# Splitting the weights of a woven projection in one piece instead of four quarters

## The reference

```python
def mem_cross_attention(q, mem_n, w_mkv):          # second block, once in each of its two layers
    k, v = jnp.split(mem_n @ w_mkv, 2, axis=-1)    # mem_n 256 x 1024, w_mkv 1024 x 1024
    ...

def swa_sink_attention(q, k, v, sinks):            # first block, layer 1: 12 heads, 4 blocks of 128 tokens
    s = jnp.einsum('bnqhgd,bnkhd->bnhgqk', qb, kband).astype(jnp.float32) * (dh ** -0.5)
    s = jnp.where(valid[None, :, None, None, :, :], s, -jnp.inf)
    m = jnp.maximum(jnp.max(s, axis=-1, keepdims=True), sink)
    p = jnp.exp(s - m)
    p = p / (jnp.sum(p, axis=-1, keepdims=True) + jnp.exp(sink - m))
    o = jnp.einsum('bnhgqk,bnkhd->bnqhgd', p.astype(v.dtype), vband)
```

## Time and profile before

| what | value |
|---|---|
| runs, median (lowest to highest) | 2280.4 us (2272.93 to 2281.29), 3 runs |
| profiled execution, its own time | 2280.4 us |
| its span in the profile | 2278.9 us |
| TensorE busy | 93% of the span |
| VectorE busy | 51% |
| ScalarE busy | 39% |
| chain that ended last, by engine | PE 77%, DVE 15%, ACT 6%, issue 1% |
| mean granted TensorE clock | 0.958 |
| sliding stage in the trace | about 795 to 934 us |

### The profile page before, as it was taken

How to read it: one execution, slowest core, us unless ns; L and a number is a source line. 1 busy time by engine, 2 the same in 40 slices (tenths; PEclk the granted TensorE clock), 3 DMA queues, 4 the chain that set the end, 5 groups by cost and what they waited for, 6 DMA issues and landing times.

```text
span 2278.9 us, 24588 instructions
## 1 busy us (share of the span) xinstructions
PE 2111.9 (93%) x9984; PEld 1716.7 (75%) x9984; DVE 1168.8 (51%) x2252; ACT 883.9 (39%) x1565; POOL 231.7 (10%) x155
## 2 busy tenths in 40 slices
PE   6998899999997999999999999999998899799787
PEld 6986688888786777788887878878776666577575
DVE  5325453333226666453332237998865248655553
ACT  5336443222124356442322222477451222456520
POOL 1000010000002000010000003766500000000000
PEclk9998599999998999999999999999999899999998
DMA  6330022233233212222222322322322312011211
GB/s 225 114 117 11 10 83 93 93 99 105 102 107 114 67 55 75 93 97 98 93 93 93 111 93 96 108 74 74 102 74 74 110 56 70 23 38 56 74 56 56
DMA packets 28800, 192.60 MB, mean 85 GB/s; under 512 B 3264, under 2 KB 3408, under 8 KB 7440
## 3 DMA queue, kind: packets, MB, share of 16 engines
q1 hardware_dynamic: 24848, 175.96, 22.5%
q0 software_dynamic: 3264, 12.99, 1.7%
q10 hardware_dynamic: 576, 2.10, 0.2%
HBM read 186.84 MB, written 4.19 MB: 84 GB/s over the span
## 4 chain that ended last, share of the span: by engine, by line
PE 77%; DVE 15%; ACT 6%; issue 1%; DMA 0%; POOL 0%; SPq 0%; DVEq 0%; POOLq 0%; ACTq 0%
PE bank L390 22%; PE bank L391 21%; PE bank L392 21%; DVE bank L1971 4%; PE bank L1660 2%; DVE WL L362 1%; PE bank L1551 1%; ACT WH L348 1%; PE bank L1090 1%; PE bank L1648 1%; PE bank L1099 1%; PE bank L1027 1%; PE bank L1561 1%; PE bank L2112 1%; PE bank L1653 1%
## 5 line engine op out<-in xcount | busy, mean ns | idle before, releaser
L390 PE MATMUL bank<-XH,WH 128*128 128x512 f32 (+1 forms) x1504 | 598.5, 398 | 25.4 <-DVE XL L551 10.3
L392 PE MATMUL bank<-XH,WL 128*128 128x512 f32 (+1 forms) x1504 | 568.5, 378 | 0.0
L391 PE MATMUL bank<-XL,WH 128*128 128x512 f32 (+1 forms) x1504 | 567.9, 378 | 0.0
L362 DVE TENSOR_TENSOR WL<-RAW,WH 128x2048 fp32r<-128x2048 f32 x128 | 293.2, 2291 | 462.8 <-ACT WH L348 462.8
L348 ACT ACTIVATE WH<-RAW 128x2048 fp32r<-128x2048 f32 x148 | 282.3, 1908 | 347.1 <-PE bank L392 341.7
L390 PEld LDWEIGHTS bank<-XH,WH 128*128 128x128 f32 x1504 | 286.8, 191 | 94.6 <-issue 24.7
L391 PEld LDWEIGHTS bank<-XL,WH 128*128 128x128 f32 x1504 | 287.1, 191 | 54.4 <-issue 5.6
L392 PEld LDWEIGHTS bank<-XH,WL 128*128 128x128 f32 x1504 | 286.3, 190 | 53.3 <-issue 0.6
L1971 DVE SCALAR_TENSOR_TENSOR bank<-conv_in,cols,bank 128x512 f32<-128x512 f32 x290 | 198.1, 747 | 1.1
L390 PE MATMUL bank<-WH,XH 128*128 128x512 f32 (+2 forms) x416 | 154.6, 372 | 9.8 <-DVE XL L551 6.3
L391 PE MATMUL bank<-WL,XH 128*128 128x512 f32 (+2 forms) x416 | 153.7, 369 | 0.0
(11 more groups left out here) (316 smaller groups left out, 3023.8 us busy)
## 6 DMA issues: line engine op xcount, KB each, us to landing
RAW<-weights SPq DMA_DIRECT2D x164, 1024.0 KB, 4.9
row_a<-rows POOLq DMA_DIRECT2D x7, 512.0 KB, 5.8
row_b<-rows POOLq DMA_DIRECT2D x6, 512.0 KB, 6.0
x_res<-x SPq DMA_DIRECT2D x1, 2048.0 KB, 16.7
kv<-mem_park POOLq DMA_DIRECT2D x2, 1024.0 KB, 5.1
out<-x_res ACTq DMA_DIRECT2D x4, 512.0 KB, 2.6
mem_tok<-mem SPq DMA_DIRECT2D x1, 1024.0 KB, 5.0
mem_tok<-mem POOLq DMA_DIRECT2D x1, 1024.0 KB, 8.4
```

The costliest lines, as they stand in the source:

```text
L362: dve.tensor_tensor(WL[j][:, :], RAW[j][:, :], WH[j][:, :].bitcast(F32), ALU.subtract).then_inc(*lo.mark())
L390: pe.matmul(ps, ah, bh, start=first, stop=False)
L391: pe.matmul(ps, ah, bl, start=False, stop=False)
L392: return pe.matmul(ps, al, bh, start=False, stop=last)
```

## The change

The quarters are no longer used in this stage. `split_act` and `lower_dve`, one whole operation each, take their place, at the entry at which the unit ends: the last of 18 entries for keys and the last but one of 16 for values, since the empty entry now stands behind each step of the values. The list keeps its 136 entries, and they alone are dealt out over the same 66 steps. The copies of the values move from an odd entry to the even one before it. The lags stay, and so do the lines that do the work. The quarters of a later stage (`gate_b`) are not touched.

```diff
-    VALUE_STEPS = 2 * KB
-    BESIDE = [(layer, unit, k) for layer in range(2) for unit in range(4)
-              for k in range(FEATURE_STEPS if unit < 2 else VALUE_STEPS)]
-    QUARTERS = {}
-    for e, (layer, unit, k) in enumerate(BESIDE):
-        if k == (FEATURE_STEPS if unit < 2 else VALUE_STEPS) - 1:
-            for q in range(4):
-                QUARTERS[e + 1 + 2 * q] = q
+    BESIDE_VALUES = [step for i in range(2) for t in range(MEMT) for q in range(4) for step in ((i, t, q), None)]
+    BESIDE = [(layer, part, k) for layer in range(2) for part, count in (("keys", 2 * FEATURE_STEPS), ("values", len(BESIDE_VALUES)))
+              for k in range(count)]
     BESIDE_LAGS = 2, 3
-    BESIDE_ENTRIES = max(QUARTERS) + 1
 
     def beside(n, lag=0):
 
-        steps, n = len(SLIDE_ORDER) - BESIDE_LAGS[1], n - lag
-        return range(BESIDE_ENTRIES * n // steps, BESIDE_ENTRIES * (n + 1) // steps) if 0 <= n < steps else []
+        steps = len(SLIDE_ORDER)
+        n = n - lag
+        at = [0] + [len(BESIDE) * (k + 1) // (steps - BESIDE_LAGS[1]) for k in range(steps - BESIDE_LAGS[1])] + [len(BESIDE)] * 8
+        return BESIDE[at[n]:at[n + 1]] if n >= 0 else []
...
-    def beside_act(e):
-        if e in QUARTERS:
-            split_quarter_act(QUARTERS[e])
-        if e >= len(BESIDE):
-            return
-        layer, unit, k = BESIDE[e]
-        u = U["mem2_kv", layer, unit]
-        if unit < 2 and k in (KB, FEATURE_STEPS - 1):
-            c = k // (FEATURE_STEPS - 1)
...
+    def beside_act(layer, part, k):
+        if part == "keys":
+            unit, k = divmod(k, FEATURE_STEPS)
+            u = U["mem2_kv", layer, unit]
+            for c in range(2):
+                if k == KB * (c + 1) + c:
...
+            if k == FEATURE_STEPS - 1:
+                split_act()
+        elif BESIDE_VALUES[k]:
+            i, t, q = BESIDE_VALUES[k]
+            if (i, q) == (1, 3):
...
+            if (t, q) == (MEMT - 1, 3):
+                split_act()
+
+    def beside_dve(layer, part, k):
+        if part == "keys" and k % FEATURE_STEPS == FEATURE_STEPS - 1:
+            lower_dve()
+        elif part == "values" and BESIDE_VALUES[k] in [(0, MEMT - 1, 3), (1, MEMT - 1, 3)]:
+            lower_dve()
```

More of the change, by code:

```diff
@@ L1445, in band, with beside_pe @@
         return P if t == 0 else 2 * P
-    VALUE_STEPS = 2 * KB
-    BESIDE = [(layer, unit, k) for layer in range(2) for unit in range(4)
-              for k in range(FEATURE_STEPS if unit < 2 else VALUE_STEPS)]
-    QUARTERS = {}
-    for e, (layer, unit, k) in enumerate(BESIDE):
-        if k == (FEATURE_STEPS if unit < 2 else VALUE_STEPS) - 1:
-            for q in range(4):
-                QUARTERS[e + 1 + 2 * q] = q
+    BESIDE_VALUES = [step for i in range(2) for t in range(MEMT) for q in range(4) for step in ((i, t, q), None)]
+    BESIDE = [(layer, part, k) for layer in range(2) for part, count in (("keys", 2 * FEATURE_STEPS), ("values", len(BESIDE_VALUES)))
+              for k in range(count)]
     BESIDE_LAGS = 2, 3
-    BESIDE_ENTRIES = max(QUARTERS) + 1
     def beside(n, lag=0):
-        steps, n = len(SLIDE_ORDER) - BESIDE_LAGS[1], n - lag
-        return range(BESIDE_ENTRIES * n // steps, BESIDE_ENTRIES * (n + 1) // steps) if 0 <= n < steps else []
-    def beside_pe(e):
-        if e >= len(BESIDE):
-            return
-        layer, unit, k = BESIDE[e]
-        u = U["mem2_kv", layer, unit]
[L1472 to L1477, removed]
+        steps = len(SLIDE_ORDER)
+        n = n - lag
+        at = [0] + [len(BESIDE) * (k + 1) // (steps - BESIDE_LAGS[1]) for k in range(steps - BESIDE_LAGS[1])] + [len(BESIDE)] * 8
+        return BESIDE[at[n]:at[n + 1]] if n >= 0 else []
+    def beside_pe(layer, part, k):
+        if part == "keys":
+            unit, k = divmod(k, FEATURE_STEPS)
+            feature_step_pe(k, U["mem2_kv", layer, unit], n=MEM, source=m2_parts, ring="beside")
+        elif BESIDE_VALUES[k]:
+            i, t, q = BESIDE_VALUES[k]
+            u, kb, high, low = U["mem2_kv", layer, 2 + i], 4 * i + q, *m2_parts
+            if (t, q) == (0, 0):
                 PE.wait_ge("split_lo", u + 1)
@@ L1481, in beside_pe @@
             mm = three_passes(bank[banks_of["mem2_v", layer, t]][:, :], high[:, kb, t * P:(t + 1) * P],
-                              low[:, kb, t * P:(t + 1) * P], WH[u % 2][:, s], WL[u % 2][:, s], kb == 0, kb == KB - 1)
+                              low[:, kb, t * P:(t + 1) * P], WH[u % 2][:, 512 * q:512 * q + 512],
+                              WL[u % 2][:, 512 * q:512 * q + 512], kb == 0, kb == KB - 1)
+            last = (t, q) == (MEMT - 1, 3)
             if kb == KB - 1:
-                mm.then_inc(*(used if t == MEMT - 1 else T).mark("full", "mem2_v", layer, t))
-            elif (t, q) == (MEMT - 1, 3):
+                mm.then_inc(*(used if last else T).mark("full", "mem2_v", layer, t))
+            elif last:
@@ L1510, in beside_dve @@
-    def beside_dve(e):
-        if e in QUARTERS:
-            lower_quarter_dve(QUARTERS[e])
+    def beside_act(layer, part, k):
+        if part == "keys":
+            unit, k = divmod(k, FEATURE_STEPS)
+            u = U["mem2_kv", layer, unit]
+            for c in range(2):
+                if k == KB * (c + 1) + c:
+                    if layer:
+                        ACT.wait_ge(*after("park", 0, "keys"))
+                    ACT.wait_ge(*after("full", u, c))
+                    act.activation(m2_keys[:, MEM * (2 * unit + c):MEM * (2 * unit + c + 1)], bank_of(u, c)[:, 0:MEM],
+                                   AF.Copy).then_inc(*A.mark("emptied", u, c))
+            if k == FEATURE_STEPS - 1:
+                split_act()
+        elif BESIDE_VALUES[k]:
+            i, t, q = BESIDE_VALUES[k]
+            if (i, q) == (1, 3):
+                if layer:
+                    ACT.wait_ge(*after("park", 0, "values"))
+                ACT.wait_ge(*after("full", "mem2_v", layer, t))
+                act.activation(m2_values[:, 512 * t:512 * t + 512], bank_of("mem2_v", layer, t)[:, :], AF.Copy).then_inc(
+                    *A.mark("emptied", "mem2_v", layer, t))
+            if (t, q) == (MEMT - 1, 3):
+                split_act()
@@ L1536, in sliding_pe @@
                 if stream == 1:
-                    beside_pe(other[k])
+                    beside_pe(*other[k])
                     continue
@@ L1584, in sliding_act @@
             for other in beside(n, BESIDE_LAGS[0]):
-                beside_act(other)
+                beside_act(*other)
     def sliding_dve():
@@ L1612, in sliding_dve @@
             for other in beside(n, BESIDE_LAGS[1]):
-                beside_dve(other)
+                beside_dve(*other)
             if n % 3 == 2 and n < 12:
```

## The result

The change costs 3.5%: 2355.5 us in the median (2347.4 to 2366.3, 4 runs) where the kernel before took 2276.8 (4 runs); the ratio is 1.035, with a 95% interval of 1.029 to 1.041. The prediction was 2295 us, with a range of 2286 to 2302. The sign was right, and the loss of 78.7 us is over five times the 14.6 that I forecast.

What follows compares the result with a forecast made beforehand. TensorE bounds the sliding stage. To 2280.4 us the prediction added 10.3 us net (12.9 of stalls less 2.6 back) and 4.8 us for falls of the clock: 2295 us, range 2286 to 2302.

Steps and rivals of the forecast that it cites:

- The bound: In the sliding stage TensorE is busy 134.5 of 137.0 us; VectorE and ScalarE have over a third of their time free.
- The lump's way to TensorE: ScalarE's whole split, then VectorE's whole operation, delay the reciprocal that TensorE's transposes await; beside keys 0.88 us late.
- Step 11: First whole operation on VectorE, ahead of a rotation, beside memory jobs: TensorE stalls 2.0 us.
- Step 20: Second place on VectorE, first token block with small jobs: TensorE stalls 2.5 us.
- Step 35: Fourth place on VectorE, beside keys: a stall of 0.88 us plus 0.48 for a copy of values, 1.4 us.
- VectorE's wait for ScalarE: VectorE idles 0.2 to 1.2 us ahead of its whole operation until ScalarE's split is ready.
- The sum of the stalls: Seven TensorE stalls ahead of its transposes in the sliding stage, 12.9 us together.
- Step 68: Last place, behind the last result, beside the transposes of `mixed`: no stall; 1.2 us if VectorE can't catch up.
- What comes back: TensorE's waits for last quarters and a reciprocal go, 1.7 us, plus savings at the stage's end: 2.6 us back.
- The clock: Four falls to half clock behind the stalls, 1.2 us each: 4.8 us; ends 0 and 12 us.
- Longer falls of the clock: Rival: half clock lengthens a step and light work keeps it low; 2303 us, chance 0.06.
- The count of short idle times: In the earlier trace five of six idle times of 2.2 to 2.5 us brought half clock, none of 1.3 to 1.5.

Runs made afterwards that it cites:

- four_whole_late: Whole operations at the last five places only (steps 35, 44, 53, 60, 68), against lists_quarters: 2280.7, 2317.7, 2331.6 and 2332.3 us.
- vector_whole: VectorE's operations whole at the place of the fourth quarter, ScalarE's splits in quarters except the last, against lists_quarters: 2354.0 us, ratio 1.033.
- lists_quarters: The changed kernel's list and pace, with quarters put back on both engines at seven of the eight places (the last stays whole): 2278.3 us, ratio 0.999.
- warm_memory: The kernel before plus 16 useless 512-column multiplies, four ahead of each of the first four jobs of the first layer's memory attention: 2277.0 us, ratio 0.999.
- pure_stall: lists_quarters plus two useless subtractions on VectorE at the end of step 21: 2320.8 us, ratio 1.018.
- one_whole_early: Against lists_quarters, also whole: ScalarE's split in step 19 and VectorE's operation in step 20, beside values: 2341.5 us, ratio 1.029.

## Why the prediction was wrong

- **The bound.** Right. TensorE sets the stage (busy 209.8 of 215 us), and VectorE's and ScalarE's free time is not the question.
- **The lump's way to TensorE.** Right, wherever the clock was at full. Step 11: 2.0 forecast, 2.15 measured. Step 20: 2.5 and 2.19. Step 35: 1.4 and, in four_whole_late, 1.25. VectorE's wait for ScalarE ahead of its operation: 0.2 to 1.2 forecast, 0.51 and 0.99 measured. Without ScalarE's lateness (vector_whole) 1.5 worked out and 1.34 measured.
- **The sum of the stalls.** 12.9 us forecast, 4.3 measured in the stage, wrong as a consequence of the clock: of seven stalls two happened. The other five found steps of 4.0 us in place of 2.2, in which the same late reciprocal is early. No run shows what the seven would have cost at full clock.
- **Step 68.** Costed at nothing, 1.2 us at worst. Wrong: TensorE stood 2.21 us there in lists_quarters and in the kernel after, and 2.1 us came of it against quarters at full clock (warm_memory). Against the profile of before it doesn't show, since that had half clock there.
- **What comes back.** 2.6 us forecast, and right in kind: the waits for WL are gone, the wait for the last result is 0.38 us in place of 0.78, and with quarters the new list's stage is 3.5 us shorter in one profile.
- **The clock.** This is the step that failed: "I take four falls. Each loses 3.0 x (1 - 9/14) = 1.1 us, a little more with its edges". That the clock falls behind a stall of 2 us was right, in both places. What a fall costs I took from the earlier trace rows, where dense multiplies of 512 columns follow and the clock is back within the next few us. I had no row of what half clock does in thin work of this stage, and set its worst at 12 us for "seven falls, some twice as long". Measured were two falls, of 10 and of 160 us, and the term is 76 us (76.8 less 4.3 of stalls, plus the 3.5 that came back). The rival "Longer falls of the clock" named this mechanism, with a chance of 0.06 and a price of 2303 us, 52 us too low. The trace of before had the warning: in the memory attention, behind an idle time of 1.07 us, the last of five within 10 us, half clock lasted 48 us. I had counted it as one of the stretches of low clock, not asked why it lasted, and for idle times I had looked at those out of dense work alone.
- **The count of short idle times.** "Of those of 1.3 to 1.5 us none was" held for dense work. In this stage stalls of 1.25 and 1.34 us were followed by half clock in three of four and four of four runs, by their times, and in one profile a stall of 0.78 us was, which in that of before was not. The two idle times of 1.3 us ahead of the stage, followed by full clock in the trace of before, were followed by half clock in eight of twelve profiles. One trace could not show this. That "even a short stall is paid twice" was my own inference; the page named beside it does not say it of stalls this short, and the runs have it both ways.

What stays open: what ends a long fall, and why one stall of a length is followed by a fall and another is not. Beside keys at the start of the stage the clock was back after 7 to 10 us, behind the second place it wasn't for 150 us or more. But values or keys are not what decides: among the same sliding jobs beside keys warm_memory had it back after 14 us, and four_whole_late kept half clock for the 48 us beside keys and 57 more. In pure_stall it came back after 99 us, in a part of the stage that doesn't look different from the part before. No run here tells why.

## What to carry to other kernels

Where TensorE is busy with thin work, read the clock as a state that the stage keeps, not as a price per idle time. Before a change that makes TensorE stand for a microsecond, ask whether the stretch behind it would bring the clock back, and look in the trace for the longest stretch at half clock and what started it. A long operation on an engine with free time can cost many times its length if it stands ahead of a short one in TensorE's loop: quarters were worth 3.5% here, nearly all of it through the clock. A profile is one execution: where a fall is chance, look at several before you count on it. A few useless dense multiplies, put where TensorE idles anyway, can be cheaper than a low clock.

## What the runs showed of the hardware that I had not expected

- One and the same stage held either clock for long: 0.50 for 157 us behind one stall of 2.19 us, 1.00 for 90 us behind the same stall and 20 dense multiplies (6.0 us).
- A TensorE that was busy 156.00 of 156 us stayed at 0.50 all the while (one_whole_early), in this stage's mix of multiplies of 64 to 512 columns.
- In this stage stalls of 1.25 us (three of four runs) and 1.34 us (four of four) were enough, and in one profile 0.78 us; out of dense work an idle time of 1.47 us, at 728 us in the trace of before, had no effect.
- Whether the clock falls behind short idle times differs between executions of the same instructions: one memory attention took 33.6 us in three profiles and about 47 us in eight.
